# The samples' attention inside the first group's second gate-up stage, and the softmax normalised by a diagonal in the turning product

## The reference

```python
logits = jnp.einsum('bnhgd,bnshd->bnhgs', qg, k_sel.astype(jnp.float32)) * HEAD_DIM ** -0.5
logits = jnp.where(valid[:, :, None, None, :], logits, -jnp.inf)
p = jax.nn.softmax(logits, axis=-1)
o = jnp.einsum('bnhgs,bnshd->bnhgd', p, v_sel.astype(jnp.float32))
...
def _swiglu(h, w_gu, w_down):
    gate, up = jnp.split(h @ w_gu, 2, axis=-1)
    return (jax.nn.silu(gate) * up) @ w_down
```

## Time and profile before

| | us |
|---|---|
| median of 3 runs | 2657.81 (2653.18 to 2659.29) |
| profiled execution, its own time | 2661.24 |
| its span, first to last instruction | 2659.4 |
| PE busy | 2541.2 (96%) |
| PE weight loads busy | 2270.7 (85%) |
| DVE busy | 1317.3 (50%) |
| POOL busy | 1253.9 (47%) |
| ACT busy | 1027.7 (39%) |
| PE psum L884 on the chain that ended last | 69% |

### The profile page before, as it was taken

One profiled execution on the slowest core, in us unless ns is written; L12 is line 12 of the kernel. 1 busy time (PEld: TensorE's weight loads), 2 busy tenths in 40 slices (PEclk: granted clock), 3 DMA queues, 4 the chain that ended last, 5 costly groups with the idle time before them and its releaser, 6 DMA issues.

```text
span 2659.4 us, 42175 instructions
## 1 busy us (share of the span) xinstructions
PE 2541.2 (96%) x15118; PEld 2270.7 (85%) x15121; DVE 1317.3 (50%) x1705; ACT 1027.7 (39%) x1534; POOL 1253.9 (47%) x634
## 2 busy tenths in 40 slices
PE   6989869999998999999999999999999999999999
PEld 5779547888886769889999999888889999999999
DVE  4567777889877646554511233621344343220234
ACT  4545654422234645644422222532232435222222
POOL 4545243664665514535544443744543334443442
PEclk8989979999998999999999999999999999999999
DMA  6546012333333142332332232332343221232232
GB/s 154 129 105 154 16 60 64 103 104 93 95 105 113 43 146 68 123 104 87 112 92 70 83 86 72 96 105 85 95 134 119 72 81 43 86 89 75 81 94 68
DMA packets 451034, 246.41 MB, mean 93 GB/s; under 512 B 86668, under 2 KB 439648, under 8 KB 449383
## 3 DMA queue, kind: packets, MB, share of 16 engines
q1 hardware_dynamic: 450927, 244.99, 31.7%
HBM read 221.23 MB, written 23.82 MB: 92 GB/s over the span
## 4 chain that ended last, share of the span: by engine, by line
PE 79%; DVE 4%; ACT 3%; POOL 2%; issue 1%; DMA 1%; SPq 0%; DVEq 0%; POOLq 0%; ACTq 0%
PE psum L884 69%; PE psum L1306 1%; PE psum L1224 1%; PE psum L1328 1%; PE psum L1318 1%; POOL w_lo L2248 1%; DVE probs_t L2844 1%; PE psum L924 1%; PE psum L1049 1%; PE psum L1436 1%; ACT probs_t L1930 1%; PE psum L1075 0%; DVE row_stats L2830 0%; PE psum L1303 0%; DVE z_rows L3129 0%
## 5 line engine op out<-in xcount | busy, mean ns | idle before, releaser
L2248 POOL TENSOR_TENSOR w_lo<-w_raw,w_hi 128x1024 fp32r<-128x1024 f32 (+1 forms) x334 | 858.4, 2570 | 1133.8 <-ACT w_hi L1614 1115.0
L884 PE MATMUL psum<-act_split,w_hi 128*128 128x288 f32 (+1 forms) x5200 | 1049.6, 316 | 5.4 <-POOL w_lo L2248 5.3
L1614 ACT ACTIVATE w_hi<-w_raw 128x1024 fp32r<-128x1024 f32 (+1 forms) x332 | 372.9, 1123 | 1318.1 <-PE psum L884 1260.7
L884 PEld LDWEIGHTS psum<-act_split,w_hi 128*128 128x128 f32 x5200 | 808.2, 189 | 50.0 <-POOL w_lo L2248 5.8
L884 PE MATMUL psum<-act_split,w_lo 128*128 128x288 f32 (+1 forms) x2600 | 647.1, 315 | 0.0
L884 PE MATMUL psum<-hidden_split,w_hi 128*128 128x288 f32 (+1 forms) x2112 | 461.5, 327 | 0.5 <-POOL w_lo L2248 0.5
L884 PEld LDWEIGHTS psum<-act_split,w_lo 128*128 128x128 f32 x2600 | 433.7, 189 | 20.0
L884 PEld LDWEIGHTS psum<-hidden_split,w_hi 128*128 128x128 f32 x2112 | 339.4, 188 | 28.2 <-issue 0.9
L884 PE MATMUL psum<-act_split_first,w_hi 128*128 128x512 f32 x1088 | 340.1, 394 | 0.5 <-POOL w_lo L2248 0.3
L884 PE MATMUL psum<-hidden_split,w_lo 128*128 128x288 f32 (+1 forms) x1056 | 288.0, 327 | 0.0
L2964 DVE TENSOR_TENSOR temps<-psum,temps 128x512 f32<-128x512 f32 (+1 forms) x88 | 63.7, 724 | 358.5 <-PE psum L884 335.5
(11 more groups left out here) (334 smaller groups left out, 2452.9 us busy)
## 6 DMA issues: line engine op xcount, KB each, us to landing
w_raw<-in_w_ffn_gate_up SPq DMA_DIRECT2D x352, 256.0 KB, 3.2
w_raw<-in_w_ffn_down SPq DMA_DIRECT2D x64, 384.0 KB, 3.6
w_raw<-in_w_ffn_down SPq DMA_DIRECT2D x64, 320.0 KB, 4.0
w_raw<-in_w_in_odd SPq DMA_DIRECT2D x64, 256.0 KB, 3.0
w_raw<-in_w_in_even SPq DMA_DIRECT2D x60, 256.0 KB, 3.9
w_raw<-in_w_out_odd SPq DMA_DIRECT2D x32, 256.0 KB, 3.2
x_rows<-in_x_prompt SPq DMA_DIRECT2D x8, 512.0 KB, 6.0
w_raw<-in_w_out_even SPq DMA_DIRECT2D x32, 128.0 KB, 3.0
```

The costliest lines, as they stand in the source:

```text
L884: mm = pe.matmul(PS[:, 2 * p + b, 0:hi - lo], w[:, p, at], x(k)[:, lo:hi], start=(k == order[0] and w is WH and x is x_hi), stop=(k == ord ...
L1614: act.activation(WH[:, p, 0:n], WR[:, p, 0:n], ACT.Copy).then_inc(S("w_hi"), 1)
L2248: pool.tensor_tensor(WL[:, p, 0:n], WR[:, p, 0:n], WH[:, p, 0:n].bitcast(F32), ALU.subtract).then_inc(S("w_lo"), 1)
```

## The change

1. The samples' attention leaves its place behind the second attention. It is spread over the 22 chunks of group 0's second gate-up stage: keys of sample b are turned ahead of block 4 of chunk 2b, logits made in chunk 2b+1, probabilities turned in chunk 2b+3, values multiplied in chunk 2b+4. One PSUM bank (6) holds both the turned keys and the turned probabilities. SP fetches the pages between the weights of that stage. The stage is written out instead of looped.
2. `pe.transpose(probs, IDENT)` becomes `pe.matmul(probs, DG)`, where DG is a 128x128 diagonal of the inverse sums that VectorE writes for each head. GpSimd's multiplications go, as do VectorE's of heads 32 to 35.
3. Tiles move: the first group's residual is fetched ahead of the end of the second attention, and group 1's residual (X) only at its end, ahead of the output projection's weights on SP.

```diff
 elif kind == "tr":
     if kk == 0:
         pe.wait_ge(S("p_norm"), 8 * t + 4 * z + 4)
     wait(pe, S("pt_lo"), kc - 1)
     for j in range(4):
-        mm = pe.transpose(PS[:, 4 + kc % 2, P * j:P * j + P], probs(8 * t + 4 * z + j)[:, P * kk:P * kk + P], IDENT)
+        hh = 8 * t + 4 * z + j
+        mm = pe.matmul(PS[:, 4 + kc % 2, P * j:P * j + P], probs(hh)[:, P * kk:P * kk + P], DG[:, hh % RING, :],
+                       start=True, stop=True)
...
 def invert(hh):
     dve.wait_ge(S("exp"), hh + 1)
+    if hh >= RING:
+        dve.wait_ge(S("p_tr"), kbase(hh // 8 - 1, hh % 8 // 4) + hh // 8)
     dve.reciprocal(MX[:, 3, c], MX[:, 2, c]).then_inc(S("inv"), 1)
-    if 32 <= hh < 36:
...
+    dve.wait_ge(S("inv"), hh + 1)
+    dve.tensor_scalar(DG[:, hh % RING, :], IDENT, MX[:, 3, c], None, ALU.mult).then_inc(S("p_norm"), 1)
...
-    pool.tensor_tensor(pr, pr, MX[:, 3, hh % 16:hh % 16 + 1].to_broadcast([P, P * (t + 1)]), ALU.mult).then_inc(S("p_norm"), 1)
...
+def sample_turn(b):
+    pe.wait_ge(S("ps_norm"), 2 * b + 2)
+    pe.wait_ge(S("ktb"), min(b + 2, DB))
+    wait(pe, S("pts"), b)
+    for j in range(NPG):
+        pe.matmul(PS[:, 6, NS * j:NS * j + NS], PRS[:, P * j:P * j + P], DGS[:], start=True, stop=True)
...
+sample = {}
+for b in range(DB):
+    sample[2 * b, 4] = lambda b=b: sample_keys(b)
+    sample[2 * b + 1, 4] = lambda b=b: sample_logits(b)
+    sample[2 * b + 3, 3] = lambda b=b: sample_turn(b)
+    sample[2 * b + 4, 6] = lambda b=b: sample_values(b)
-gate_up(phase("gu", 0, 0, 1))
+gate_up(phase("gu", 0, 0, 1), sample, FH)
...
+def sample_aside(c):
+    b, odd = divmod(c, 2)
+    if odd == 0 and b < DB:
+        page_keys(b)
+    if odd and 1 <= b <= DB:
+        sample_turned(b - 1)
+    if odd and b < DB:
+        sample_exponentials(b)
...
 sp.wait_ge(S("pv_mm"), kbase(8, 0))
-sp.dma_start(XH[:], x0_dram).then_inc(S("first_in"), 16)
-sp.wait_ge(S("pvs_mm"), 2)
-sp.dma_start(YH[:], y0_dram).then_inc(S("first_in"), 16)
+sp.dma_start(YT[:], y0_dram[:, 6:8, :]).then_inc(S("tail_in"), 16)
+sp.dma_start(X[:], x_dram).then_inc(S("second_in"), 16)
```

More of the change, by code:

```diff
@@ L668, in in_stage, with pages @@
                         sp.dma_start(outs["new_pool_sample"][0, b, BUF - DT:BUF], XNS[DT * b:DT * b + DT, 1, :]).then_inc(S("st_out"), 16)
[L670 to L676, removed]
+            def pages(b):
+                if b > 1:
+                    sp.wait_ge(S("kt_ps"), b - 1)
+                if b > 3:
+                    sp.wait_ge(S("pvs_mm"), b - 3)
+                for i in range(NPG):
+                    page = sp.value_load(PGT[0:1, NPG * b + i:NPG * b + i + 1], min_val=0, max_val=DB * NPG * 5 // 4 - 1)
+                    for to, name in ((KP[:, b % 2, i, :], "cache_k"), (VP[:, b % 4, i, :], "cache_v")):
+                        rows = ins[name][0].rearrange("n s h d -> n s (h d)")[ds(page, 1)].rearrange("a s d -> (a s) d")
+                        sp.dma_start(to, rows).then_inc(S(f"pages_in{b % 2}"), 16)
             def first_queries(g):
@@ L820, in _ @@
             rest(phase("dn", 0, 0, 0))
-            channel(0, 0, (1,))
+            ph = phase("gu", 0, 0, 1)
+            head(ph)
+            pages(0)
+            for i in range(1, FH):
+                some(ph, i, i + 1)
+                if i < DB:
+                    pages(i)
+            head(phase("dn", 0, 0, 1))
+            rest(phase("dn", 0, 0, 1))
             store_mixed(((0, 4), (4, 6)))
@@ new lines, in sample_keys, with sample_logits @@
+            def sample_keys(b):
+                pe.wait_ge(S(f"pages_in{b % 2}"), 128 * (b // 2 + 1))
+                wait(pe, S("ktb"), b)
+                wait(pe, S("pts"), b - 1)
+                for j in range(NPG):
+                    mm = pe.transpose(PS[:, 6, P * j:P * j + P], KP[:, b % 2, j, :], IDENT)
+                mm.then_inc(S("kt_ps"), 1)
+            def sample_logits(b):
+                pe.wait_ge(S("ktb"), b + 1)
+                pe.wait_ge(S("iqz"), 3)
+                pe.wait_ge(S("qz0"), 3)
+                wait(pe, S("exps"), b)
+                for bank, lo, hi, keys in ((4, 0, PAST, KTB[:]), (5, PAST, KCOL, KT[:, SEQ:SEQ + NS])):
+                    pe.matmul(PS[0:NS, bank, 0:hi - lo], EB[:, b, :], MKS[:, lo:hi], start=True, stop=False)
+                    mm = pe.matmul(PS[0:NS, bank, 0:hi - lo], QZ[:, b, :], keys, start=False, stop=True)
+                mm.then_inc(S("qks_mm"), 1)
@@ L1992, in gate_up @@
                 warm(ACT.Silu)
-                loop(ph, take, early, GU_PAIRS[g] if aside else 0, aside)
+                loop(ph, take, early, pairs or (GU_PAIRS[g] if aside else 0), aside)
             def down(ph, mp):
@@ L2207, in _ @@
             down(phase("dn", 0, 0, 0), norm_at(0, 1))
-            gate_up(phase("gu", 0, 0, 1))
+            for j in range(4):
+                heads_of_sample(j)
+            gate_up(phase("gu", 0, 0, 1), False, sample_aside, FH)
             down(phase("dn", 0, 0, 1), norm_at(0, 1))
@@ L2397, in attend @@
                         continue
-                    hh = 8 * t + z
-                    if t == 4 and z < 4:
-                        continue
-                    wait(pool, S("p_norm"), hh)
                     if z == 4 and t % 4 < 3:
@@ L2859, in attend, with sample_mask, sample_guest @@
                             invert(pending.pop(0)[0])
-            def attend_sample():
-                for b in range(DB):
+            def sample_mask():
+                dve.memset(QZ[:], 0.0).then_inc(S("qz0"), 1)
+                dve.wait_ge(S("top"), 2 * (SMALL + 17))
+                dve.tensor_scalar(MKS[:], SCS[:, 0:KCOL], SPLITTER, MASK, ALU.is_gt, ALU.mult).then_inc(S("qz0"), 1)
+            def sample_guest(c):
+                b, odd = divmod(c, 2)
+                if odd and b < DB:
```

250 lines of the change are left out of this document (101 added, 149 removed).

## The result

| | before | after |
|---|---|---|
| median of 4 runs each | 2658.55 | 2711.26 (2708.78 to 2714.28) |
| ratio (95% interval) | | 1.0206 (1.019 to 1.0222) |
| profiled execution, its own time | 2661.24 | 2711.43 |

Applied to the 2657.8 us on which the forecast stands, the ratio gives 2712.6: 0.6 above the range of 2664 to 2712, and 21 above the value. The sign and most of the steps were forecast; a cost was missing. Busy time of the changed kernel by stretch (columns as in the earlier trace rows): the first attention, the second gate-up stage of group 0 with the samples in it, the second attention from its first turn, and the head of group 1's output projection.

The account below looks back on a forecast made before the run. TensorE was taken to set the gate-up stage's pace, with some idle time in both attentions. Terms -38.6 + 39.5 + 12.6 + 13.0 + 7.0 = +33.5 us gave a median of about 2691, range 2664 to 2712.

Parts of the forecast that it names:

- A: Samples' own stage goes, and the output projection behind it starts at full clock: -38.6 us.
- B: Group 0's second gate-up stage: the samples' products come back there, 4.94 us per sample, +39.5 us.
- C: Gate-up stage: TensorE waits 1.80 us for the page keys' copy at seven turns, +12.6 us.
- D: Second attention: turning by diagonal products costs 18.1 us, partly offset by gains from waits and multiplications, +13.0 us.
- E: First attention: turning products cost 9.0 us, GpSimd's waits give 4, VectorE's diagonals show 2; +7.0 us.
- F: Transfers: page fetches stay hidden, and X ahead of the output projection's weights costs 0 to +3; taken as 0.
- Rival 2: Interleaved gate-up stage: ScalarE's or VectorE's part of the sample's chain comes later, longer waits; 2704 to 2722, chance 0.15.
- Rivals 3, 4 and 5: 3: attention hides products, 2664, chance 0.13; 4: diagonal product one pass, 2657, 0.05; 5: one pass at column rate, 2648, 0.07.

Follow-up runs that it names:

- the run with the keys ahead: The changed kernel with the page keys' copy moved ahead of the table load and silu on ScalarE; 2691.72 us, ratio 1.0127.

## Why the prediction was off

The profiled times differ by 50.2 us where 33.5 were summed. The terms as measured add to 51.7; the rest is the work behind them.

| term | forecast | measured | by |
|---|---|---|---|
| A samples' own stage, low clock behind it | -38.6 | -38.6 | stage -36.6; from the projection's first product to the one with root_rstd 4.78 us instead of 6.74 |
| B products in gate-up | +39.5 | +43.1 | stage without waits |
| C waits | +12.6 | +11.0 | seven waits |
| low clock behind the waits | not there | +12.5 | the stage's rest (6.4 to 12.3 in five other runs) |
| D second attention | +13.0 | +13.3 | stretches |
| E first attention | +7.0 | +6.2 | stretches |
| F transfers | 0 | +4.2 | projection: 59.7 against 55.5 |

**C failed, by what it left out: the clock behind its waits.** Its 1.80 us per wait were 1.57: the chain of w_hi, load, silu and copy on ScalarE, the seven places and the copy as the last to end are all as worked out. But the term priced a wait at its length. Term A of the same sum had read that the clock stood at 0.52 behind the samples' stage, where TensorE "had waited twice and done small products before", and C set up just this seven times in a stage that had run at 1.00. The runs put 12.5 us on it in the profiled execution, more than the waits themselves, and none where nothing is waited for. Without it the same terms add to 39.2, about 2697 as a median, well inside the range. Rival 2 (2708) came nearest, with its time but not its mechanism: no further engine was late. The Trainium skill ("TensorE: Matmul & The Clock Gate", A second HAM failure mode: psum-queue depth-cycling) tells of another kernel in which frequent short idle spells between groups of products make the clock swing between its two levels; the trace agrees, with one wait of 1.57 us in the pair from 692.96 and a clock of 0.77 there.

**B** was 3.6 short. At full clock, in the run with the keys ahead, one sample's products take 0.36 (keys), 1.74 (logits), 1.28 (turn) and 1.29 (values), 4.67 against 4.94 forecast. But a pair there takes 16.25 us, 0.70 more than these and its 10.88 of weights' products: the block right behind narrow products lasts 0.78 to 0.90 us instead of 0.68, four times per sample, 0.56 of the 0.70. Over eight samples the products came out 2.2 us cheaper than forecast and the interruptions, which had no price, cost 5.6. The turn is ten instructions, as said; as a transpose it is 0.84 us cheaper per sample (6.7 over eight).

**D** held: products 17.65 (forecast 18.1), the multiplications gone -6.6 and the diagonals +2.3, together -4.3 (forecast 3.5 + 1.5 gained). Its "upper bound" of 12.6 us of waits for both attentions had left out the 3.6 us for VectorE's own multiplications. Each figure is the difference of two executions, with clocks of 0.98 and 0.95 in these stretches for the products. The turn's rows are x8 with 0.80 us to the next, in the changed kernel near 1040 us:

```profile
1037.62 1.05 PE L1329 MATMUL psum<-inverse_diagonals,probs_long_b 128*128 128x128 f32 x8
1038.42 0.94 PE L1340 MATMUL psum<-probs_t,values_split 128*128 128x512 f32 x3
1039.20 1.05 PE L1329 MATMUL psum<-inverse_diagonals,probs_long_b 128*128 128x128 f32 x8
```

Rivals 3, 4 and 5 fall with it.

**E** came out right by errors that cancel. Products +2.4 instead of +9.0, in a stretch in which TensorE idled for 21 us; GpSimd's freed time -0.4 instead of -4, since the 9.1 us of waits for it came back as waits for VectorE (probs_t from 10.6 to 14.6 us, row_stats from 0 to 4.4) and 1.0 for ScalarE; the diagonals +4.2 instead of +2: VectorE, busy for 53.6 of 74 us before, got 8.4 us more, and half of it showed. That the sum came out right is luck. Each step depends on the order in which the parts are undone, and the clock differs between these runs (0.74 to 0.87), so the split is good to some 2 us.

**F** was set to 0 with 3 as its end; it was 4.2. The residual was priced at its duration alone (9.4 us; it took 11.3), against weights wanted 11 us behind the attention's end. But SyncE issued it and, behind it, the weights only from 1049.2, behind the attention's end, and both landed in sequence: w_hi could start at 1063.28, and w_lo comes behind it. Of the 4.2 us some 3.2 are the longer wait; behind it the clock fell once more, to 0.55 from 1066.8 to 1069.7, which F had left out as C did.

## What to carry to other kernels

A short wait put into a stretch in which TensorE is gapless costs more than its length, since the clock can fall behind it: look first whether the granted clock there is 1.00, and then place the guest work so that nothing is waited for, which here took one copy moved ahead of a table load, or the turn three blocks later. Moving work from a stage with hardly any idle time into another without idle time won nothing here even without a wait. The waits for an engine say little by themselves of what freeing it gives: 9.1 us of them gave 0.4 in the first attention, where VectorE was late as well, and 7.1 gave 6.6 in the second.

## What the runs showed of the hardware

- Seven waits of about 1.6 us in one stage cost 0, 1.6, 3.1 or 4.6 us of low clock each, and 6.4 to 12.5 in all in six executions of the same instructions; at 2.00 us it was 21.5, and without waits 0 in all four kernels that had none.
- In these kernels narrow products among wide ones slow the block of wide products behind them by 0.1 to 0.2 us even at full clock.
- The same work near 2260 us took 34.2 or 37.2 us, with a clock of 0.95 or 0.86, and the stage with its seven waits varied by 6.1 us: differences of that size between single executions of these kernels mean nothing by themselves.
